# Rows of the older window tiles laid on partitions by row within the group first, then by group, in the dilated layer's buffer attention

## What is computed

```python
DIL_PAIRS = ((128, 1), (512, 4), (2048, 16))
def _dilated_gather(q, k_all, v_all, q_idx, d, span):
    idx = q_idx[:, None] - d * jnp.arange(span + 1)[None, :]
    valid = idx >= 0
    kg, vg = k_all[:, jnp.maximum(idx, 0)], v_all[:, jnp.maximum(idx, 0)]
    s = jnp.einsum('nqhd,nqkhd->nqhk', q, kg).astype(f32) * ATTN_SCALE
    ...
stats = [_dilated_gather(q, k_all, v_all, q_idx, d, w // d) for w, d in DIL_PAIRS]
y = _mix_branches(stats)
```

## Time and profile before

| | before |
|---|---|
| median of three runs | 2959.71 us |
| the profiled execution | 2957.88 us |
| its span, first to last instruction | 2956.2 us |
| TensorE busy | 2372.1 us (80%) |
| VectorE busy | 1441.8 us (49%) |
| ScalarE busy | 856.3 us (29%) |
| GpSimd busy | 367.9 us (12%) |
| granted TensorE clock, mean | 0.862 |
| DMA, mean over the span | 133 GB/s |

### The profile page before, as it was taken

The page is one execution under the profiler, slowest core; times in us unless marked ns, Lnnn a source line. Parts: engine busy times, 40 slices in busy tenths (PEclk is TensorE's granted clock), DMA queues, the critical chain, the costliest instruction groups (busy, mean ns, idle before and its releaser), DMA issues. The chain is left out here.

```text
span 2956.2 us, 65217 instructions
## 1 busy us (share of the span) xinstructions
PE 2372.1 (80%) x26389; PEld 1807.3 (61%) x26389; DVE 1441.8 (49%) x2258; ACT 856.3 (29%) x1547; POOL 367.9 (12%) x566
## 2 busy tenths in 40 slices
PE   5779687888777489638899997995887777799998
PEld 1347366767645278326677775763476665577776
DVE  0123467767714744265554226236765664644223
ACT  0022354444311322012333223212643332433222
POOL 0000023333310000001111000012411111011000
PEclk9669698888778689568999998998977878899999
DMA  8862149999842000111233231321199992133221
GB/s 291 293 204 72 33 130 321 354 312 344 282 133 70 0 3 4 15 28 46 77 87 86 86 92 56 93 65 64 36 260 274 288 266 78 51 88 90 85 86 60
DMA packets 326053, 391.85 MB, mean 133 GB/s; under 512 B 26630, under 2 KB 227793, under 8 KB 325803
## 3 DMA queue, kind: packets, MB, share of 16 engines
q1 hardware_dynamic: 293514, 278.23, 30.7%
q0 software_dynamic: 32288, 110.12, 11.7%
HBM read 377.58 MB, written 10.70 MB: 131 GB/s over the span
## 5 line engine op out<-in xcount | busy, mean ns | idle before, releaser
L721 PE MATMUL bank<-yT,WH 128*128 128x288 f16 x3200 | 531.3, 289 | 44.5 <-DVE yT L584 34.1
L774 DVE SCALAR_TENSOR_TENSOR WL<-wring,WH 128x1024 f16<-128x1024 f32 x194 | 255.1, 1319 | 290.2 <-ACT WH L754 290.2
L721 PEld LDWEIGHTS bank<-yT,WH 128*128 128x128 f16 x3200 | 315.8, 99 | 130.0 <-issue 38.3
L1213 DVE TENSOR_TENSOR KL<-bank,KH 128x512 f16<-128x512 f32 x416 | 282.7, 687 | 215.3 <-ACT KH L1189 208.2
L1109 PE MATMUL bank<-cst,kslot 128*128 128x128 f32 x1664 | 318.1, 323 | 65.7 <-DMA kslot<-in_state_dil_k 36.8
L1189 ACT CAST KH<-bank 128x512 f16<-128x512 f32 x416 | 243.1, 585 | 407.7 <-PE bank L1109 407.7
L721 PE MATMUL bank<-uT,WH 128*128 128x288 f16 x2048 | 337.5, 288 | 11.0 <-DVE WL L774 11.0
L721 PE MATMUL bank<-yT,WL 128*128 128x288 f16 x1600 | 331.0, 289 | 0.0
L754 ACT ACTIVATE WH<-wring 128x1024 f16<-128x1024 f32 x194 | 203.4, 1053 | 323.5 <-PE bank L721 220.9
L1109 PEld LDWEIGHTS bank<-cst,kslot 128*128 128x128 f32 x1664 | 208.2, 161 | 95.4 <-DMA kslot<-in_state_dil_k 41.3
L721 PEld LDWEIGHTS bank<-uT,WH 128*128 128x128 f16 x2048 | 201.4, 98 | 63.3 <-issue 11.6
(11 more groups left out here) (393 smaller groups left out, 3608.3 us busy)
## 6 DMA issues: line engine op xcount, KB each, us to landing
kslot<-in_cache_fox_k SPq DMA_DIRECT2D x256, 256.0 KB, 5.3
vslot<-in_cache_fox_v POOLq DMA_DIRECT2D x256, 256.0 KB, 5.5
wring<-in_ada_w SPq DMA_DIRECT2D x96, 512.0 KB, 5.2
kslot<-in_state_dil_k SPq DMA_DIRECT2D x80, 512.0 KB, 10.6
vslot<-in_state_dil_v POOLq DMA_DIRECT2D x80, 512.0 KB, 15.3
wring<-in_mlp_up SPq DMA_DIRECT2D x64, 512.0 KB, 4.1
wring<-in_mlp_down SPq DMA_DIRECT2D x64, 512.0 KB, 3.7
wring<-in_ev_w_in SPq DMA_DIRECT2D x26, 512.0 KB, 3.8
```

Source lines behind the costliest of these rows:

```text
L721: last = nc.tensor.matmul(bank[b + h][:, 0:HALF], w[s % 2][:, c, :], x[:, s % parts * KC + c, h * HALF:(h + 1) * HALF], start=(s % parts = ...
L774: nc.vector.scalar_tensor_tensor(WL[s % 2][:, :, :], w[:, :, :], WSCALE, WH[s % 2][:, :, :], ALU.mult, ALU.subtract).then_inc(w_free, 1)
L1213: nc.vector.tensor_tensor(KL[i][:, :], turned[n % NT][:, :], KH[i][:, :], ALU.subtract).then_inc(lo_out, 1)
```

## The change

The order of the rows of an early tile on the partitions. Before, partition p holds row p mod 8 of group p div 8. After, partition p holds row p div 16 of group p mod 16. The source pattern becomes 8 rows with a step of 1024 floats, then 16 groups with a step of 16384, then 1024 floats. The destination is as before. `dilated_keys()` gives the new positions, so the constant `lc_past` has its rows in the new order. No instruction is added or removed, and no wait.

```diff
 def dilated_keys():
 
-    early = (np.arange(96)[:, None] * 16 + np.arange(8)[None, :]).reshape(6, P)
+    early = (np.arange(96).reshape(6, 1, 16) * 16 + np.arange(8)[None, :, None]).reshape(6, P)
     return np.concatenate([early, 1536 + np.arange(512).reshape(4, P)])
@@ def load(eng, n, dst, done):
                     if tile < 6:
-                        a = early[seq:seq + 1, tile * 16:(tile + 1) * 16, 0:8, :].rearrange("a g r n -> (a g) r n")
+                        a = early[seq:seq + 1, tile * 16:(tile + 1) * 16, 0:8, :].rearrange("a g r n -> (a r) g n")
                     else:
                         a = src[seq:seq + 1, 1536 + (tile - 6) * P:1536 + (tile - 5) * P, :].rearrange("a w n -> (a w) n")
                     eng.dma_start(dst[:, :], a).then_inc(done, 16)
```

## The result

The changed kernel takes 3071.26 us (median; 3060.62 to 3074.66), the kernel before beside it 2960.09 us. The ratio is 1.0357, 95% interval 1.0332 to 1.0381: about +106 us, or 111 us from median to median. The forecast was 3065 us.

The account below looks back on a forecast made before the run. DMA transfers were taken to bound the stage. Early keys 26.2, early values 13.1 and late tiles 10.4 make 49.7 us a sequence instead of 36.6; x 8 is 105 us more, giving 3065 us, range 2990 to 3172.

Parts of the forecast that it names:

- The bound: In the stage from 2133 to 2437 us, DMA transfers set the time, at share 0.97, with TensorE busy 229.4 us.
- The number of engines: Early keys on SP's queue use 8 engines; values on GpSimd's queue alternate between the halves.
- The sum: On the keys' half of the engines, a sequence takes 49.7 us instead of 36.6, x 8 = 105 us more.
- the term of the late tiles: In each sequence, 64 packets of late tiles at 163 ns take 10.4 us, as before.
- The term of the keys: Early keys on 8 engines: 96 packets x 273 ns = 26.2 us a sequence, before 13.1.
- the change heals nothing: Engines writing early tiles still collide in pairs at the destination, so a packet stays at about 273 ns.
- the faster rival: Early tiles on 8 engines run at 163 ns a packet: 22 us gained, 2938 us; faster had chance 0.13.
- the forecast's own signs of being wrong: Small packets staying at 16, early keys alone at 205 GB/s, or POOL's bursts 63 us apart.
- The term of the values: Early values on 16 engines or on the halves by turns: 48 packets on average, 13.1 us a sequence, as before.
- Waits: TensorE's waits for keys (`kslot`) in the stage grow by about 100 us.
- DMA share: The stage's DMA share falls from 0.97 to about 0.72, 295 us of 16 engines' work in 409 us.
- The cause of slow early tiles: Engines meeting in pairs on the write side would halve 403 GB/s to about 202; a far DRAM pitch costs little.

Follow-up runs that it names:

- The run with 4 rows first: Kernel before with early tiles loaded as 4 rows by 32 groups, row first (source pattern 4 x 32 x 1024): 3209.9 us, ratio 1.0841.
- The values by halves: Kernel before with only early values in the new order, each tile loaded by two transfers, to partitions 0 to 63 and 64 to 127: 2979.45 us, ratio 1.0052.

## Why the prediction was right, point by point

*The bound.* DMA sets the stage: right. A sequence went from 37 us between the bursts to 49.0, and the kernel by about as much as the stage.

*The number of engines.* 8 for SP's queue: right, by 896 small packets and by the share near 0.5 with early keys alone. The run with 4 rows first and the one whose late tiles are 8 runs follow the same count (704, 1024). The rule of the Trainium skill ("DMA: Bandwidth & Descriptors", on the increment of 16) holds in this case's traces, as far as the number goes. That the values are not all on one half holds too: the share of 1.05 with early values alone, and what happened when two transfers of 8 engines got different partitions. The records do not name an engine, so the turn by turn is inferred, not seen.

*The sum.* It came out at 105 us for a measured 104 in the stage. The direction and the half of the engines that carries the loss were right, but the prices were not, and it was luck that they made up for each other. With the stage means, taken as the same on both halves, and values that go to the halves by turns, the keys' half carries 128 packets of keys x 228 ns and 80 of values x 280 ns in a sequence, 29.2 + 22.4 = 51.6 us; the stage has 409/8 = 51.1. The forecast's own terms are 26.2 + 5.2 = 31.4 us for keys and 13.1 + 5.2 = 18.3 for values: keys came out about 2 us lower, values about 4 higher. These means hold early and late tiles together. Part of the 4 is the term of the late tiles, taken at 163 ns "as before", which no stretch of 6 us of the kernel after reaches on both queues.

The term of the keys, 96 packets x 273 ns where there were 48, was to give 13.1 us more a sequence, 105 us in all. Alone it gave about 73. In the stretches with early keys alone the packets on 8 engines took 232 to 239 ns, and in some stretches 155 to 165. The step that failed is "the change heals nothing": part of the faster rival was true, now and then. One of the forecast's own signs of being wrong came up so, a stretch with early keys alone at 205 GB/s: the one from 2240 to 2246 us has 212. The one from 2159 to 2165 has 137, nearer to the 120 forecast. What decides when the engines meet stays open; the run on 4 engines had 156 ns.

The term of the values was to be nothing, "13.1 us, as before". Alone it gave about 66 us. That no half gets all of them was right, their price was not: 458 ns for 273 where they run alone, 293 for 233 in the mean of that run's stage. The working had taken the meeting in pairs from the keys and not asked what happens when both halves carry the same pattern at the same time. The values by halves fit that, with the reserve made there.

Together the two give 106 us by the same reckoning, and not 139. The stage means show where they overlap: values in the new order raise the price of SP's packets when the keys have the old order (256 for 232 ns), and not when they have the new one (228 in the change, and 227 with keys alone, 36.0% of 2136 to 2540 us). Why, no run separates.

*Waits.* TensorE's waits for `kslot` were to grow by about 100 us. They grew by 21, and those for `vslot` by 69. The same error, seen from the engine.

*DMA share.* 0.72 was forecast, 0.79 measured: dear packets count as busy.

*The cause of slow early tiles.* The forecast leaned to the write side by rows 10 and the factor of two. The late tiles of 16 runs (238 GB/s) against those 64 KB apart (404) show that the split decides. The Trainium skill, "SBUF — State Buffer", on the DMA port swizzle, says that 4 neighbouring partitions and the 4 that lie 32 on share one port. What the runs show is in keeping with it: blocks of 4 partitions in the pattern go at 416 GB/s, an outermost extent of 16, which would give an engine 8 neighbouring partitions, at 240, and 128 partitions walked by both halves at 143. Neither the ports nor the partitions that an engine wrote are in any row, so this reason stays an inference.

## What to carry to other kernels

The outermost extent of a DMA pattern is a performance choice even when the bytes, the packets and their sizes are the same: 128 x 4 KB went at 416 and 240 GB/s with 32 and 16 outermost, and at 105 with 4 (SP's queue alone). In this kernel 32 groups of 4 rows went as fast as 128 single rows; where rows are free to be permuted, that order adds no instruction and no byte. And a forecast that comes out right in sum is not yet right: a run with each term alone showed two errors of opposite sign.

## What the runs showed that was not expected

On GpSimd's queue a transfer on fewer engines has extra packets of 4 bytes: an early tile has 144 at an extent of 8 and, from 29952 - 10240 - 32 x 16 = 19200 over 48 tiles, 400 at an extent of 4. That is 16 + 8 x 16 and 16 + 12 x 32: as if each idle engine got one for every packet that a working one got; that reading fits the counts and no row names the engines. SP's queue has none of these, only 8 and 4 small packets a tile. The run by halves has more of them than the run with values alone (18432 and 17664 packets on that queue, 10240 of data) and lost 15 us where that one lost 66, so they are not what costs.

Engines at share 1.05 moved 143 GB/s, others at a share of 1.02 moved 416. A DMA share near 1 says that engines are occupied, not that they are fast; the rate beside it has to be read with it.

A contiguous source written in two dimensions is merged back when the program is built, so an experiment on the split needs a gap in the source.
